# Sample attention of a hybrid decoder step: one pipeline of 8-page chunks in 16 array tiles, key loads on SP, value loads on ScalarE's queue

## What is computed

```python
# branch B, for each sample: two softmaxes per head, their difference times the values
s = einsum('bqhmd,bshmd->bhmqs', q * DH_B ** -0.5, k)      # past and new keys, m = 0, 1
p = softmax(s)
o = einsum('bhqs,bshe->bqhe', p[:, :, 0] - lam * p[:, :, 1], v)
o = rmsnorm(o, subln_g, 1e-5) * (1.0 - lam_init)
# branch A: only the 256 keys with the best indexer scores count
_, sel = lax.top_k(score, topk)
s = einsum('bqgrd,bqkgd->bqgrk', q * DH_A ** -0.5, kv[:, :, :, 0])
o = einsum('bqgrk,bqkgd->bqgrd', softmax(s), kv[:, :, :, 1])
```

## Time and profile before

| | us |
|---|---|
| median of 3 runs (lowest, highest) | 4287.01 (4286.02, 4287.13) |
| the profiled execution | 4291.84 |
| its span, first to last instruction | 4290.3 |
| sample_attend in it: first load issued at 1462.35, first load of `tail` at 2737.61 | 1275 |
| mean granted clock of PE over the span | 0.896 |

### The profile page before, as it was taken

How to read it: one execution, slowest core, us unless ns; L and a number is a source line. 1 busy time by engine, 2 the same in 40 slices (tenths; PEclk the granted TensorE clock), 3 DMA queues, 4 the chain that set the end, 5 groups by cost and what they waited for, 6 DMA issues and landing times. The chain is left out here.

```text
span 4290.3 us, 63118 instructions
## 1 busy us (share of the span) xinstructions
PE 3336.9 (78%) x19602; PEld 2146.4 (50%) x19602; DVE 1466.1 (34%) x2999; ACT 889.8 (21%) x1700; POOL 399.2 (9%) x738
## 2 busy tenths in 40 slices
PE   8998994697810278778777777399399999899868
PEld 4444563476710245455455444265266666566545
DVE  2222797576378533233233233121511111000131
ACT  1111200464500134323323422001100000000011
POOL 0000000000200122322222232100000000000000
PEclk9998897799855689999999999699699999999989
DMA  5233122200500377887887787711011111101011
GB/s 191 74 100 117 40 76 75 83 1 11 178 10 0 115 228 243 289 284 257 269 284 265 250 296 258 283 37 35 24 29 39 39 39 30 45 27 40 13 51 49
DMA packets 375010, 512.06 MB, mean 119 GB/s; under 512 B 44178, under 2 KB 222514, under 8 KB 374291
## 3 DMA queue, kind: packets, MB, share of 16 engines
q1 hardware_dynamic: 330898, 376.79, 26.6%
q0 software_dynamic: 44032, 134.26, 9.9%
HBM read 463.94 MB, written 47.00 MB: 119 GB/s over the span
## 5 line engine op out<-in xcount | busy, mean ns | idle before, releaser
L1629 PE MATMUL gu_b<-ta_z,gu_w 128*128 128x352 f32 x2112 | 626.6, 460 | 25.1 <-DMA gu_w<-w_gate_up 25.1
L1629 PEld LDWEIGHTS gu_b<-ta_z,gu_w 128*128 128x128 f32 x2112 | 402.0, 190 | 250.2 <-issue 27.4
L1298 PE MATMUL sa_turn_b<-sa_ident,sa_ring_b 128*128 128x128 f32 x2048 | 325.3, 290 | 78.6 <-DVE sa_prob L1512 33.1
L1413 ACT COPY sa_key_b<-sa_turn_b 128x512 f32<-128x512 f32 x512 | 296.6, 590 | 404.8 <-PE sa_turn_b L1298 404.7
L1298 PEld LDWEIGHTS sa_turn_b<-sa_ident,sa_ring_b 128*128 128x128 f32 x2048 | 249.2, 148 | 182.3 <-issue 157.9
L213 PE MATMUL pr_acc<-pr_w,pr_u_t 128*128 128x512 f32 (+1 forms) x864 | 326.6, 539 | 0.0
L1629 PE MATMUL dn_b<-ta_act_t,dn_w 128*128 128x352 f32 x1056 | 314.2, 461 | 11.8 <-DMA dn_w<-w_down 11.8
L1484 DVE COPY sa_key_a<-sa_turn_a 128x512 f32<-128x512 f32 x128 | 88.6, 692 | 602.1 <-PE sa_turn_a L1304 602.1
L1215 POOL DMA_DIRECT2D sa_ring_a<-cache_a_kv x448 | 240.8, 537 | 559.5 <-DVE sa_held_a L1486 301.0
L1350 PE MATMUL sa_o<-sa_ring_b,sa_p_now 128*8 128x128 f32 x4096 | 221.7, 278 | 75.0 <-DMA sa_ring_b<-cache_b_kv 72.8
L1629 PEld LDWEIGHTS dn_b<-ta_act_t,dn_w 128*128 128x128 f32 x1056 | 201.3, 191 | 124.6 <-DMA dn_w<-w_down 12.4
(11 more groups left out here) (284 smaller groups left out, 4066.2 us busy)
## 6 DMA issues: line engine op xcount, KB each, us to landing
sa_ring_b<-cache_b_kv SPq DMA_DIRECT2D x800, 256.0 KB, 4.0
sa_ring_a<-cache_a_kv POOLq DMA_DIRECT2D x448, 128.0 KB, 3.8
sa_ring_b<-cache_b_kv POOLq DMA_DIRECT2D x224, 256.0 KB, 5.6
gu_w<-w_gate_up SPq DMA_DIRECT2D x44, 512.0 KB, 4.6
dn_w<-w_down SPq DMA_DIRECT2D x8, 1408.0 KB, 6.6
pr_w<-w_in SPq DMA_DIRECT2D x5, 2048.0 KB, 15.7
heads_t<-pr_heads SPq DMA_DIRECT2D x9, 1024.0 KB
gate_t<-sel_gate SPq DMA_DIRECT2D x16, 528.0 KB, 3.0
```

What stands on the lines that cost most here:

```text
L1298: ins = pe.transpose(turn_b[j % 2][:, h, :], ring_b[:, slot, h * P:(h + 1) * P], ident[:])
L1413: nc.scalar.copy(key_b[:, n % 2, :, j % QUAD, :], turn_b[j % 2][:]).then_inc(b_copied[j % 2], 1)
L1629: ins = pe.matmul(banks[st][o][:, 0:PIECE], w[s][o][:, j, :], moving[:, j, piece * PIECE:(piece + 1) * PIECE], start=(j == 0), stop=(j == ...
```

## The change

Everything in `sample_attend` but its output is written anew. A chunk is 8 pages; the 64 chunks of the 8 samples form one pipeline, written out instruction by instruction with no hardware loop. In step s PE scores chunk s-1 and multiplies the values of chunk s-10. Keys and values have rings of 16 pages each, branch A apart from branch B. DVE transposes keys in 32x32 blocks; PE's score products run in sixteen 32x32 tiles of the array. SP issues both key loads of a page, ACT's queue both value loads. In `sample_select` the transposes and `bias_t` fall away; 16 DMAs store `hit` as `sel_rows`, read back in sample_attend 4 loads per half sample. The 10 small loads at the phase's start become 33.

```diff
-        bias_t = ph.sb("bias_t", [P, NB, NQ, NPG])
+        a["sel_rows"] = nc.dram_tensor("sel_rows", (2, 4, 2, PAIRS, NQ, 8, PAGE), F32, kind="Internal").ap()
...
+            for c in range(2):
+                for half in range(2):
+                    for j in range(4):
+                        first = c * 64 + half * 32 + j * 8
+                        dst = a["sel_rows"][half, j, c].rearrange("p t g s -> g (p t) s")
+                        sp.dma_start(dst, hit[first:first + 8, :, 0:PAGE]).then_inc(sel_stored, 16)
...
-            for b in range(NB):
-                sp.dma_start(bias_t[b * NQ:(b + 1) * NQ, b, :, PAGES], a["new_bias"][b % 2, (b // 2) * NQ:(b // 2 + 1) * NQ, :].rearrange("q s -> s q"),
-                             allow_slow_non_contiguous=True).then_inc(nb_in, 16)
...
-            for g in range(PAIRS):
...
-                for t in range(NQ):
-                    ins = pe.transpose(turn[g % 2][:, t, :], hit[:, g * NQ + t, 0:PAGE], ident[:])
...
+    CH = 8
+    PER = PAGES // CH
+    CHUNKS = NB * PER
+    LAG = PER + 2
+    RING = 2 * CH
...
+            sp.wait_ge(pages_in, 16)
+            for s in range(CHUNKS):
+                if s % 4 == 0:
+                    load_sel(s // 4)
+                for n in range(s * CH, s * CH + CH):
+                    if n >= RING and n % 4 == 0:
+                        sp.wait_ge(turned_b, (n - RING) // 4 + 1)
+                    if n >= RING and n % CH == 0:
+                        sp.wait_ge(turned_a, s - 1)
+                    page = sp.value_load(pages[0:1, n:n + 1])
+                    sp.dma_start(ring_k[:, n % RING, :], rows_of(cache_b, page, 0)).then_inc(k_in[s % 2], 16)
+                    sp.dma_start(ring_ka[:, n % RING, :], rows_of(cache_a, page, 0)).then_inc(ka_in[s % 2], 16)
...
+            def scores(c):
...
+                for d in range(4):
+                    for k in range(4):
+                        rows = slice(32 * k, 32 * k + 32)
+                        for h in range(H_B):
+                            ins = pe.matmul(s_bank[32 * h:32 * h + 32, k, 0:CH * 32], q_pad[rows, d, j, h, :], key_b[rows, c % 2, :, 4 * h + d, :],
+                                            start=(j == 0 and d == 0), stop=(j == 3 and d == 3), tile_position=(32 * k, 32 * h), skip_group_check=True)
...
+            for s in range(1, CHUNKS + LAG):
+                if s - 1 < CHUNKS:
+                    scores(s - 1)
+                    if s % PER == 0:
+                        new_scores(s // PER - 1)
+                if s >= LAG:
+                    values(s - LAG)
+                if s % PER == 0 and s <= CHUNKS:
+                    spread_top(s // PER - 1)
+                if s % PER == 1 and s > PER:
+                    b = s // PER - 1
+                    if b:
+                        combine(b - 1)
+                    if b < NB:
+                        turn_prob(b)
+                        sum_up(b)
...
+            def prob_out(b):
+                if b:
+                    act.wait_ge(pv_done, b)
...
+            def load_values(v):
+                for n in range(v * CH, v * CH + CH):
+                    if n >= RING:
+                        act.wait_ge(v_used, n - RING + 1)
+                    page = act.value_load(pages[0:1, n:n + 1])
+                    act.dma_start(ring_v[:, n % RING, :], rows_of(cache_b, page, 1)).then_inc(v_in[v % 2], 16)
+                    act.dma_start(ring_va[:, n % RING, :], rows_of(cache_a, page, 1)).then_inc(va_in[v % 2], 16)
...
+            for s in range(1, CHUNKS + LAG):
+                if s % 4 == 0 and s <= CHUNKS:
+                    b_out(s // 4 - 1)
+                if s % PER == 0 and s <= CHUNKS:
+                    exps(s // PER - 1)
+                if s % PER == 1 and PER < s < CHUNKS + PER:
+                    prob_out(s // PER - 1)
+                if 0 <= s - LAG + 1 < CHUNKS:
+                    load_values(s - LAG + 1)
...
+            def turn_keys(c):
+                dve.wait_ge(k_in[c % 2], (c // 2 + 1) * CH * 16)
+                if c >= 2:
+                    dve.wait_ge(scored, c - 1)
+                slot = c * CH % RING
+                for i in range(0, CH, 4):
+                    nc.vector.transpose(key_b[:, c % 2, i:i + 4].rearrange("p g n s -> p (g n s)"),
+                                        ring_k[:, slot + i:slot + i + 4, :].rearrange("p g e -> p (g e)")).then_inc(turned_b, 1)
...
+            for s in range(CHUNKS + LAG):
+                if s < CHUNKS:
+                    turn_keys(s)
+                if s % 4 == 0 and 0 < s <= CHUNKS:
+                    a_out(s // 4 - 1)
+                if s % PER == 0 and 0 < s <= CHUNKS:
+                    if s < CHUNKS:
+                        set_q(s // PER)
+                    softmax_shift(s // PER - 1)
+                if s % PER == 1 and s > PER:
+                    b = s // PER - 1
+                    if b:
+                        finish(b - 1)
+                    if b < NB:
+                        invert(b)
```

More of the change, by code:

```diff
@@ L1162, in sample_attend @@
         rms = ph.sb("rms", [P, 2, H_B * NEW])
-        turn_b = [ph.ps(f"turn_b{c}", [P, H_B, P]) for c in range(2)]
-        turn_a = ph.ps("turn_a", [P, QUAD, P])
-        s_bank = [ph.ps(f"s{c}", [P, QUAD * P]) for c in range(2)]
-        back = ph.ps("back", [P, QUAD, P])
-        last = ph.ps("o", [P, 512])
-        o_b, o_a, o_t = last[:, 0:P], last[0:QA, P:2 * P], last[:, 2 * P:3 * P + QA]
-        sums = last[:, 3 * P + QA:3 * P + QA + Q]
+        s_bank = ph.ps("s", [P, 4, 512])
+        turn = [ph.ps(f"turn{c}", [P, 4, P]) for c in range(2)]
@@ new lines, in sample_attend @@
+        k_in, ka_in, v_in, va_in, sel_in = ([ph.sem(f"{n}{c}") for c in range(2)] for n in ("k_in", "ka_in", "v_in", "va_in", "sel_in"))
+        turned_b, turned_a, scored, half_scored, b_read, a_read = (
+            ph.sem(n) for n in ("turned_b", "turned_a", "scored", "half_scored", "b_read", "a_read"))
+        q_ready, q_set = ph.sem("q_ready"), ph.sem("q_set")
+        new_scored, top_ready, top_turned, rows_ready, spread, shifted, exped = (
+            ph.sem(n) for n in ("new_scored", "top", "top_turned", "rows", "spread", "shifted", "exped"))
@@ L1265, in _, with load_sel @@
+            assert len(small) == 33
             for dst, src in small:
                 sp.dma_start(dst, src).then_inc(small_in, 16)
-            stream(sp, [(lambda j, v: v == 0 or j not in V_BY_POOL, ring_b, b_in, rows_b), (lambda j, v: v == 0 and j in BY_SP, ring_a, a_in, rows_a)])
+            def load_sel(n):
+                b, half = divmod(n, 2)
+                if n >= 2:
+                    sp.wait_ge(a_read, n - 1)
+                for j in range(4):
+                    sp.dma_start(sel[32 * j:32 * j + 32, n % 2].rearrange("p g k s -> p (g k s)"),
+                                 a["sel_rows"][half, j, b % 2, b // 2].rearrange("t g s -> t (g s)").partition_broadcast(8)).then_inc(sel_in[n % 2], 16)
@@ new lines, in exps @@
+                ins.then_inc(exped, 1)
+            def prob_out(b):
+                if b:
+                    act.wait_ge(pv_done, b)
+                for n in range(GROUPS):
+                    m = b * GROUPS + n
+                    act.wait_ge(p_turned, m + 1)
+                    if n == GROUPS - 1:
+                        nc.scalar.copy(prob_new[:], turn[m % 2][0:NEW, 0:2, :]).then_inc(p_copied, 1)
+                    else:
+                        half, g, r = n // 4, n // 2 % 2 * 4, n % 2
+                        nc.scalar.copy(prob_t[:, half, g:g + 4, r, :], turn[m % 2][:]).then_inc(p_copied, 1)
```

589 lines of the change are left out of this document (259 added, 330 removed).

## The result

The changed kernel takes 4349.61 us (median of 4 runs, 4340.24 to 4355.42), the one before 4287.07 (4 runs beside it). The ratio is 1.0141, with a 95% interval of 1.0118 to 1.0164: slower by 1.4%. The forecast was 4321, slower, in 4190 to 4440. The profiled execution is the fastest of the four, 4340.24 us; its span of 4338.5 is 48.2 us over that of before. I compare these two traces. The medians are 62.5 us apart: the profiled execution before lies 4.8 us over its median, the one after 9.4 us under its own.

The account below looks back on a forecast made before the run. Key pass bound by PE and its handshake, value pass by loads; afterwards DMA, or issue where one stream runs. Phase +29, last combination +2, sample_select's end +3: +34 on 4287.0, 4321 us; range 4190 to 4440.

Parts of the forecast that it names:

- the likeliest case: Whole kernel: period hardly moves (153 for 154 us), head and end lose, 34 us slower, 4321 us; chance 0.45.
- The price of a page: DMA time for one page's key and value loads, both streams mixed: 1.95 us, or 7.8 us per half-chunk.
- The price of an issue: Issuing a page's two loads on SP or ACT: 1.5 us, between 1.4 and 1.7; sets the pace where one stream runs.
- they go at the transfer's pace: Rival, head and end: keys alone and values alone run at 0.98 us per page, -62 us, 4259; chance 0.05.
- The gap: Turn of each sample: both rings stop, 41 us (34 to 48) with only 16 us of DMA work.
- the next value loads stand behind the exponentials: Turn of a sample: value loads wait behind ACT's exponentials, so the first is issued 10 us after.
- keys fill the gap: Rival, turn of a sample: SP's key loads run through the gap, six times 15.6 us, -94, 4227; chance 0.25.
- All of it lies beside 15.6 us of DMA per chunk; I cost it at nothing there: Compute per chunk: DVE's key turns 5.5 us, PE's scores and value products, all covered by DMA, adding nothing.
- The first softmax: Head, first sample: turn, scores 3.6, copies and maximum, chain and exponentials uncovered, 22 us in all, ending at +140.
- The eighth period: Last full period: four key half-chunks instead of seven, 130 us, ending at +1154.
- Code fetch: Rival: straight code's instruction fetches hold loads back and PE waits, 2 us in each of 56 chunks, 4430; chance 0.12.
- ACT's issue: Rival: issuing loads costs more on ACT than SP, setting the pace from 1.95 us per page; 4650; chance 0.08.

Follow-up runs that it names:

- s1_loads_first: Changed kernel with ACT issuing each step's value loads first, ahead of score copy, exponentials and probability copies: 4152.32 us, 0.9673 of the kernel before.
- s3_ends_shared: Changed kernel with first sample's branch-A key loads issued by ACT and last sample's branch-A value loads by SP: 4295.34 us, 1.0015 of the kernel before.
- s5: Changed kernel with value loads issued first only in the step of the exponentials: 4261.45 us, 0.9933 of the kernel before.
- s6: Changed kernel with value loads issued first only in the step of the probability copies: 4261.34 us, 0.9934 of the kernel before.
- s12_mid_sample: Changed kernel with value loads issued first only in the step of the mid-sample score copy: 4305.26 us, 1.0036 of the kernel before.
- s8_pe_busy: Changed kernel with 40 zero products on PE per step, ahead of each chunk's value products: 4434.93 us, 1.0334 of the kernel before.
- s7: Changed kernel with DVE taking out scores and making the first sample's softmax shift before turning chunk 8's keys: 4347.23 us, 1.013 of the kernel before.

## Why the prediction was right, and where not

The sign, the range and the likeliest case were right: the period hardly moved, and the loss lies in the head and, most of it, in the end. Inside the period the total was met by luck, as said below. Term by term, from +0 (a turn, T0, is the first product of chunk 8B-10: 1742.3, 1893.4, ... 2502.7, 2644.5):

| | forecast | measured |
|---|---|---|
| first key load | +19 | +19.1 |
| first value load | +147 | +154.7 |
| to the first turn (T0) | 112 | 117.3 |
| five periods | 765 | 760.4 |
| the eighth | 130 | 141.8 |
| from the last T0 to the last product | 139 | 132 |
| sum | +1293 | +1306 |
| stores of sample_select and before | +3 | +8 |

- **The price of a page** (1.95 us in a mix) was right to 1%: with no stall left, s1_loads_first has 124.7 us for 64 pages.
- **The price of an issue** was 1.33 on SP and about 1.4 on ACT, under the 1.5 I took. s3_ends_shared shows that the ends were bound by it, together worth 54 us. The rival that they go at the transfer's pace is out. Since the issue was cheaper than I took it, the end came 7 us under the forecast.
- **The gap.** I had the next value load 39 us after the turn (36.3: 1893.4 to 1929.7) and 41 us in all (43.6 until SP went on). s5 and s6 show that both of its halves stand in ACT's queue order, 11 to 13 us per sample each, as the step "the next value loads stand behind the exponentials" said.
- **Two errors around the gap cancelled, by luck.** I had one half-chunk of keys in the gap; SP issued sixteen pages there, two half-chunks, from 1892.6 to 1915.5, so the rival "keys fill the gap" was right in part: DMA's share in the 43.6 us was 0.69, not half or less. And I costed everything between the gaps at nothing beside DMA; the copy of the scores in mid-sample stopped the value loads for 10.5 us, and s12_mid_sample got 44 us back from it. The step that failed is "All of it lies beside 15.6 us of DMA per chunk; I cost it at nothing there": true of the work, not of the loads queued behind the work's wait. An estimate from the two windows of the period, with 1.05 as full: DMA lost 43.6 x (1 - 0.69 / 1.05) = 15 us in the gap and 106.7 x (1 - 0.96 / 1.05) = 9 us outside it. The forecast had 41 - 16 = 25 us and nothing. The sum was right, the places were not.
- **The first softmax** was mis-sized: 22 us forecast, 33 measured from the last chunk's turn (1585.73) to the end of the exponentials. PE's scores took 8.6 us instead of 3.6 (1590.3 to 1598.9, granted clock 0.83, 1.5 us of it "issue"). The clock is the smaller part of that: in s8_pe_busy the same scores took 7.2 us at 1.00, 1.6 of it "issue", still twice the forecast. So the price of the sixteen tiles was mis-sized. And DVE waited until 1600.2 for the keys of chunk 8 and turned them, 5.7 us, ahead of taking out the scores. s7 shows that moving the latter alone wins nothing.
- **The eighth period** was 12 us longer than forecast (value products of chunks 46 and 54, at 2502.7 and 2644.5). Its next value load came 41.5 us after the turn (2544.2), 5 us later than at 1893, and the mid-sample stall is in it too; no run took it apart.
- **Code fetch** did not show as the rival had it. PE did wait for "issue", 10.7 us in the period of 1893 to 2044, but s1_loads_first has 14 us of it in a period of 125 with DMA full, so that most of it is covered. Some stands on the path: 2.5 us right ahead of the turn at 1893.3, 1.9 us in the scores that the mid-sample copy waits for. The profile doesn't say what this wait is, and no run removes it.
- **ACT's issue** is not dearer than SP's by more than 0.1 us a page.
- **The signs.** The first key load came as said, the first value load 8 us late. In mid-phase the rest of the period had 315 GB/s where I had named 370 or more, and the end 223 where I had named 340. Both figures contradict the forecast's own sum: fourteen half-chunks of 2.6 MB in 112 us are 328 GB/s, and eight pages in 12 us are 218.
- **The size.** Of the 62.5 us between the medians, 48 are explained by the trace; the 14 us by which the two profiled executions lie nearer together are not. The forecast was 34.

## What to carry to other kernels

A load belongs at the head of its engine's step, or on an engine that waits for nothing else: the changed kernel and s1_loads_first make the same transfers, and where they stand behind other work's waits decided over 197 of 4350 us. When a pipeline is costed by "this is covered by DMA", ask of each covered instruction whether a DMA issue stands behind it, and what that instruction waits for. Where only one stream runs, at a head or an end, compare the time of an issue with that of its transfer, and let an idle queue take half.

## What the runs showed of the hardware

- Two full queues that mix key and value loads with 2 KB and 512-byte rows moved 346 to 347 GB/s on ACT and SP, share 1.05, and 340 GB/s on POOL and SP, share 1.02 (1991 to 2364). In 1 us slices with no selection loads (1940 to 1980 in s1_loads_first) the rate stood at about 364.
- Blockwise 32x32 transposes of float32 on DVE take 2.29 us for 2048 elements per partition, 1.12 ns per element; the rows of before have 1.08 for an elementwise operation.
- The mean granted clock of 1905 to 2065 was 0.70 with PE busy 73 us, 0.79 with 104 and 0.93 with 136. The median record of a 128x128 value product was 421 ns in the changed kernel and 273 ns with 40 added products, the lower and the upper of the two levels (1.2 and 2.4 GHz).
- Loads with a broadcast of eight outermost drained at 218 GB/s and half of the engines' time when almost alone (1486 to 1492 in s1_loads_first); among full queues the rate fell to 252 GB/s for 4.5 us. Leaving 7 x 1.05 MB of them out saved 21 us.
- One load of 256 KB a page is issued in 0.81 us on SP, a page of 256 and 64 KB in 1.33.
